# Weight halves split one block sooner at three passages, and the last head's sum of squares moved up behind a quarter of the first output half

## The chip and the metric

The kernel runs on one core of a Trainium2 chip. PE (TensorE) multiplies, ACT (ScalarE), DVE (VectorE) and POOL (GpSimd) do the elementwise work, and SP issues most transfers. Each engine works through its own instructions in order and waits on semaphores for the others. The metric is the device time of one execution in microseconds, median of three runs. The profile gives each engine's records in time, the granted clock of PE, and what ended each wait.

## What is computed

Two transformer blocks on a `[512, 1024]` fp32 activation. The first block is a hybrid mixer (gated linear attention with four heads, plus banded attention) and a feed-forward part; the second has an attention and pooling mixer and then a convolution mixer. The change touches four joints of this chain:

```python
o_a = o_a * lax.rsqrt(jnp.mean(o_a * o_a, axis=-1, keepdims=True) + NORM_EPS)   # per GLA head
o_a = (o_a.reshape(B, L, ...) * jax.nn.silu(ga)).astype(u.dtype)
mix = jnp.concatenate([o_a, o_s], axis=-1) @ w_out                              # output halves
h = h + rmsnorm(mix, norm_mix_post)                                             # first passage
z = rmsnorm(h, norm_mlp_pre) @ w_up
ff = jnp.square(jax.nn.relu(z)) @ w_down
h = h + rmsnorm(ff, norm_mlp_post)                                              # second passage
...
y = even_mixer(rms_norm(x, pre_norm[0]), ...)
x = x + rms_norm(y, post_norm[0])                                               # third passage
h = rms_norm(x, pre_norm[1]); proj = h @ w_in                                   # odd mixer
```

## The kernel before

**Products in three parts.** Every fp32 operand is split into a high part (fp32r) and the rest: `a*b` becomes three matmuls, hi by hi, lo by hi, hi by lo (`mm3`, L702 to L704). So every weight chunk has to pass ACT (`hi`, L1362: `wh` from `wl`) and then DVE (`lo`, L1768: `wlr = wl - wh`). A weight chunk is 1024 rows by 512 columns and comes in two pieces of four 128-row tiles; each piece is one transfer of 1 MB, one ACT copy and one DVE subtraction. Two slots of buffers alternate, chunk `n` in slot `n % 2`; a slot is loaded again when the chunk two before it has been multiplied. PE waits for a piece in `weights(n, half)`, before the first matmul that reads it.

**Tiles.** 512 tokens are four blocks of 128. A tile of a chunk is 24 matmuls of 512 columns: 12 for half 0 (tiles k 0 to 3), 12 for half 1.

**Output of the first mixer.** `w_out` is multiplied in two chunks, `N_O0` and `N_O1`. Its input has eight row tiles: 4 to 7 come from the banded attention and are there early, 0 to 3 are the four GLA heads. So `N_O0` runs half 1 for all four blocks first (48 matmuls), then half 0. Head 3 is the last to be finished: ACT squares it into `sq`, PE adds the squares over the channels with a matmul of ones (`gla_sum(3)`, L912, result in `ps7`), ACT makes the inverse root with Ln and Exp (`head_scale(3)`, L1507, L1508, into `eb`), DVE scales (`gla_normed(3)`, L1989), ACT applies Silu to the four gates `ga` (L1541, which needs another table than Ln and Exp), DVE multiplies (L2011), ACT copies out the high half `act_hi` (`halves`, L1356), and DVE subtracts the low half `act_lo` (L1738). PE's half 0 waits for these low halves, tile by tile. After the Silu the kernel loads the Ln/Exp table again (`exp_ln_tables`, L1305).

**A passage** is the stretch in which a chunk's output becomes the input of the next stage: `s` is 0, 1, 2 for the first mixer to the feed-forward part, that part to the second mixer, and the second mixer to the third. Per block `b`, ACT (`boundary_blocks`) runs `half_square` (L1376: sum of squares of the second output half), `post_scale` (L1383, L1385), `pre_scale` (L1391 to L1396: sum of squares of the new residual) and `hi_turned` (L1403: high half of the transposed block). DVE runs `half_gained` (L1778 or L1780), `new_resid` (L1795), `lo_turned` (L1812) and `normed` (L1804: the block `un`), in the second passage also `add_down` (L1825). PE transposes the normed block (`turn_block`, L840) between halves of its tiles: blocks 0 and 1 in tiles 2 and 3 of the old chunk, blocks 2 and 3 in tiles 0 and 1 of the new one (in the third passage blocks 2 and 3 stand ahead of the new chunk). In `psT` there is room for one turned block, so `turn_block(s, b)` also waits for `lo_turned(s, b - 1)`. In the same loops both engines split the first chunk of the next stage (`following`): ACT its two pieces in blocks 1 and 2, DVE in blocks 2 and 3. The loop order written in the source is the order of the engine.

```python
if b in (1, 2):                # ACT, before: behind post_scale, ahead of pre_scale
    hi(following, b - 1)
if b >= 2:                     # DVE, before: behind new_resid, ahead of lo_turned
    lo(following, b - 2)
```

Of the kernel before, what the change touches and what calls it, by code (L numbers as in the profile page):

```python
# [209 lines left out]
def block_kernel(nc, a, out):  # L210
    ctx = ExitStack()
    with ctx:
# [45 lines left out]
        o1 = m1("o1", [P, KT, TOK])  # L258
# [440 lines left out]
        def _(pe):  # L699
# [397 lines left out]
            pe.wait_ge(evac_done, E_END)  # L1097
            for half in (1, 0):
                weights(N_O0, half)
                if half == 0:  # L1100
                    gla_sum(3)
                for b in range(NBLK):
                    for k in range(4 * half, 4 * half + 4):
                        if b == 0:
                            pe.wait_ge(act_lo_done, 8 + (k - 4 if half else 4 + k) + 1)
                        last = mm3(acc[:, b, :], act_hi[:, k, b * P:(b + 1) * P], act_lo[:, k, b * P:(b + 1) * P],
                                   wh[0][:, k, :], wlr[0][:, k, :], half == 1 and k == 4, half == 0 and k == 3)
                    if half == 0:
                        last.then_inc(wtile_done, 1)
# [190 lines left out]
        def _(act):  # L1300
# [105 lines left out]
            def boundary_blocks(s, following):  # L1406

                for b in range(NBLK):
                    half_square(s, 1, b)
                    post_scale(s, b)  # L1410
                    if b in (1, 2):
                        hi(following, b - 1)
                    pre_scale(s, b)
                    if b >= 1:
                        hi_turned(s, b - 1)
                hi_turned(s, NBLK - 1)
# [122 lines left out]
            head_scale(3)  # L1539
            for h in range(4):  # L1540
                act.activation(ga[:, h, :], ga[:, h, :], ACT.Silu).then_inc(silu_done, 1)  # L1541
            exp_ln_tables()
            halves(o1, (0, 1, 2, 3), lambda e, k: e.wait_ge(og_gated, k + 1))

            hi(N_O1, 0)
            hi(N_O1, 1)
# [163 lines left out]
        def _(dve):  # L1710
# [116 lines left out]
            def boundary_blocks(s, following):  # L1827

                for b in range(NBLK):
                    if s == 1:  # L1830
                        add_down(3, 1, b)
                    half_gained(s, 1, b)
                    new_resid(s, b)
                    if b >= 2:
                        lo(following, b - 2)
                    if b >= 1:
                        lo_turned(s, b - 1)
                    normed(s, b)
                lo_turned(s, NBLK - 1)
# [389 lines left out]
```

## Time and profile before

| | |
|---|---|
| runs before | 1124.20, 1126.48, 1126.49 us; median 1126.48 |
| profiled execution | 1125.93 us, of which the span of the core is 1124.1 |
| PE busy | 1033.6 us, 92% of the span, 4847 matmuls |
| DVE, ACT, POOL busy | 52%, 42%, 15% |
| mean granted PE clock | 0.96 of full speed |
| PE's longest waits | 10.8 us at the start, 7.4 ending at 25.6, 7.6 at 259.8, 4.4 at 667.5, 5.6 at 874.4, 4.3 at 1064.7 |

How to read it: the span runs from the first to the last instruction; 1.8 us lie around it. A row of the timeline gives start, duration, engine, line, operation and names; what stands in brackets is how long the engine was idle before it and what ended the idle time. A matmul record is longer than the distance to the next start, since matmuls are pipelined. The granted clock has two levels, 1.2 GHz (0.5) and 2.4 GHz (1.0); a record of a 512-column matmul is 0.39 us long at the higher and 0.63 us at the lower one. First output half 0 begins at 259.78 us; the first passage lies at 279 to 312 us, the second at 639 to 677, the third at 848 to 878.

### The profile page before, as it was taken

How to read it: one execution, taken by the hardware profiler on the slowest of the kernel's cores; microseconds unless marked ns; L12 is line 12 of the kernel's file. 1: busy time of each engine (PE TensorE's matmuls, PEld its weight loads, DVE VectorE, ACT ScalarE, POOL GpSimd, SP SyncE). 2: the span in 40 equal slices, each digit the busy share in tenths (PEclk: the TensorE clock that was granted, in tenths of full speed). 3: DMA queues.
4: the chain of work that ended last, by engine and by line, in shares of the span. 5: the costliest groups of instructions: out<-in, count | busy, mean ns of one | idle time of the engine just before them, and what ended most of it. 6: DMA issues, size and time to landing. Idle time of an engine off the chain costs nothing.

```text
span 1124.1 us, 12285 instructions
## 1 busy us (share of the span) xinstructions
PE 1033.6 (92%) x4847; PEld 824.7 (73%) x4847; DVE 584.4 (52%) x768; ACT 468.5 (42%) x765; POOL 170.0 (15%) x131
## 2 busy tenths in 40 slices
PE   3899999997999999999999979989898899979897
PEld 2677677886788888888888868767677667657676
DVE  5436665235744234333344463366556397777853
ACT  3325562135533334134123354234355557556541
POOL 2200101000000000000000000022000189886300
PEclk8999999998999999999999999989999799999989
DMA  6532102034221252233224214302033222210301
GB/s 213 73 122 76 38 1 76 1 113 150 76 76 75 75 187 75 75 109 116 76 75 149 76 38 132 141 1 75 2 136 120 68 76 76 75 54 27 145 1 75
DMA packets 55823, 93.91 MB, mean 84 GB/s; under 512 B 2581, under 2 KB 23958, under 8 KB 55638
## 3 DMA queue, kind: packets, MB, share of 16 engines
q1 hardware_dynamic: 53648, 90.61, 23.3%
q10 hardware_dynamic: 2118, 2.52, 1.6%
q8 instruction: 39, 0.64, 0.2%
q14 instruction: 18, 0.15, 0.0%
HBM read 90.76 MB, written 2.36 MB: 83 GB/s over the span
## 4 chain that ended last, share of the span: by engine, by line
PE 55%; DVE 8%; ACT 4%; issue 3%; POOL 1%; DMA 1%; SPq 0%; DVEq 0%; POOLq 0%; ACTq 0%
PE acc L702 17%; PE acc L703 17%; PE acc L704 16%; DVE wlr L1768 2%; ACT wh L1362 2%; DVE psT L2113 1%; POOL pacc L1295 1%; PE psT L861 1%; DMA wl<-in_c_w_in_dram 1%; PE ps L861 1%; PE ps L993 1%; DVE rt L1795 1%; DVE act_lo L1812 1%; ACT junk L1391 1%; PE psT L978 1%
## 5 line engine op out<-in xcount | busy, mean ns | idle before, releaser
L1768 DVE TENSOR_TENSOR wlr<-wl,wh 128x2048 fp32r<-128x2048 f32 (+1 forms) x66 | 149.9, 2276 | 96.4 <-ACT wh L1362 96.4
L702 PE MATMUL acc<-act_hi,wh 128*128 128x512 f32 x464 | 187.9, 405 | 1.7 <-DVE act_lo L1812 1.4
L704 PE MATMUL acc<-act_hi,wlr 128*128 128x512 f32 x464 | 182.3, 393 | 0.0
L703 PE MATMUL acc<-act_lo,wh 128*128 128x512 f32 x464 | 182.1, 392 | 0.0
L1362 ACT ACTIVATE wh<-wl 128x2048 fp32r<-128x2048 f32 (+1 forms) x66 | 123.7, 1880 | 61.2 <-DMA wl<-in_w_up_dram 35.1
L702 PE MATMUL acc<-wh,act_hi 128*128 128x512 f32 x320 | 131.3, 410 | 19.0 <-DVE act_lo L1738 7.6
L703 PE MATMUL acc<-wlr,act_hi 128*128 128x512 f32 x320 | 127.6, 399 | 0.0
L704 PE MATMUL acc<-wh,act_lo 128*128 128x512 f32 x320 | 127.6, 399 | 0.0
L1295 POOL TENSOR_TENSOR pacc<-pacc,prod 128x512 f32<-128x512 f32 x80 | 117.5, 1469 | 28.6 <-ACT prod L1644 16.1
L702 PEld LDWEIGHTS acc<-act_hi,wh 128*128 128x128 f32 x464 | 88.4, 191 | 21.7 <-DVE act_lo L1812 1.8
L703 PEld LDWEIGHTS acc<-act_lo,wh 128*128 128x128 f32 x464 | 88.3, 190 | 19.1 <-issue 1.7
L704 PEld LDWEIGHTS acc<-act_hi,wlr 128*128 128x128 f32 x464 | 87.9, 190 | 19.0
L703 PE MATMUL acc<-wlr,hid_hi 128*128 128x512 f32 x256 | 100.8, 394 | 0.0
L702 PE MATMUL acc<-wh,hid_hi 128*128 128x512 f32 x256 | 100.5, 393 | 0.0
L704 PE MATMUL acc<-wh,hid_lo 128*128 128x512 f32 x256 | 99.4, 388 | 0.0
L702 PEld LDWEIGHTS acc<-wh,act_hi 128*128 128x128 f32 x320 | 61.9, 194 | 34.9 <-DVE act_lo L1738 9.3
L702 PE MATMUL acc<-act_hi,w_hi 128*128 128x512 f32 x152 | 65.5, 431 | 10.8 <-DVE act_lo L1730 7.4
L1276 POOL MEMSET uu<- 128x64 f32 x1 | 0.2, 157 | 475.5 <-PE acc L704 475.5
L703 PEld LDWEIGHTS acc<-wlr,act_hi 128*128 128x128 f32 x320 | 62.3, 195 | 13.0 <-issue 0.7
L704 PEld LDWEIGHTS acc<-wh,act_lo 128*128 128x128 f32 x320 | 61.9, 193 | 13.5
L1644 ACT ACTIVATE prod<-glu,taps 128x512 f32<-128x512 f32 x88 | 60.0, 716 | 13.7 <-POOL pacc L1295 13.0
L2113 DVE SCALAR_TENSOR_TENSOR psT<-glu,taps,psT 128x512 f32<-128x512 f32 x83 | 59.7, 750 | 4.7 <-PE psT L861 4.4
(221 smaller groups left out, 1536.8 us busy)
## 6 DMA issues: line engine op xcount, KB each, us to landing
wl<-in_w_up_dram SPq DMA_DIRECT2D x16, 1024.0 KB, 6.3
wl<-in_w_down_dram SPq DMA_DIRECT2D x16, 1024.0 KB, 6.3
raw<-in_w_in_dram SPq DMA_DIRECT2D x18, 512.0 KB, 4.8
wl<-in_a_w_in_dram SPq DMA_DIRECT2D x8, 1024.0 KB, 6.2
wl<-in_c_w_in_dram SPq DMA_DIRECT2D x16, 512.0 KB, 6.2
wl<-in_w_out_dram SPq DMA_DIRECT2D x4, 1024.0 KB, 6.2
wl<-in_ab_w_out_dram SPq DMA_DIRECT2D x4, 1024.0 KB, 7.4
wl<-in_c_w_in_dram SPq DMA_DIRECT2D x4, 1024.0 KB, 6.4
```

Source lines behind the costliest of these rows:

```text
L702: pe.matmul(dst, hi, x_hi, start=first, stop=False)
L703: pe.matmul(dst, hi, x_lo, start=False, stop=False)
L704: return pe.matmul(dst, lo, x_hi, start=False, stop=last)
L861: last = pe.matmul(vacc(t, 0), diag[:, t % 2, m, :], glu[:, t % 4, j:j + TOK], start=m == 0, stop=m == PE_TAPS - 1)
L978: last = pe.transpose(psTf[:, (2 * b + j) * P:(2 * b + j + 1) * P], LG[layer][:, i % 2, j, 1 + b * P:1 + (b + 1) * P], ident[:, :])
L993: last = pe.matmul(ps6[:, 64 * j:64 * j + 64], PT[layer][:, (2 * b + j) * P:(2 * b + j + 1) * P], VTOK[layer][:, kb, 64 * g:64 * g + 64], ...
L1295: pool.tensor_tensor(pacc[:, t % 2, :], pacc[:, t % 2, :], prod[:, g % 4, :], ALU.add)\
L1362: act.activation(wh[slot][:, kk, cols], wl[slot][:, kk, cols], ACT.Copy).then_inc(whi_done, 1)
L1391: act.activation(junk[:, :], rt[:, b, :], ACT.Square, accum_out=ssq[:, s, 16 + b:17 + b])\
L1644: act.activation(prod[:, g % 4, :], glu[:, t % 4, j:j + TOK], ACT.Copy, scale=taps[:, t, j:j + 1])\
L1768: dve.tensor_tensor(wlr[slot][:, kk, cols], wl[slot][:, kk, cols], wh[slot][:, kk, cols].bitcast(F32), ALU.subtract).then_inc(wlo_done, 1)
L2113: ins = dve.scalar_tensor_tensor(out=sums, in0=src, scalar=taps[:, t, m:m + 1], in1=sums, op0=ALU.mult, op1=ALU.add)
```

## The change

Three edits.

1. PE: `gla_sum(3)` stood between half 1 and half 0 of `N_O0`, behind 48 matmuls. It now stands inside half 1, behind the 12 matmuls of block 0; 36 matmuls that ran ahead of it now run behind it (in PE's instruction order it goes from row 667 to row 631).
2. ACT: the reload of the Ln/Exp table behind the four Silu now stands behind the four `act_hi` copies.
3. At the three passages, ACT copies piece 0 of the next chunk in block 0 (ahead of `pre_scale` in the first two, behind it in the third) and piece 1 in block 1; DVE subtracts them in blocks 1 and 2. Before, it was blocks 1 and 2 for ACT, 2 and 3 for DVE.

No instruction is added or taken away.

```diff
             for half in (1, 0):
                 weights(N_O0, half)
-                if half == 0:
-                    gla_sum(3)
                 for b in range(NBLK):
+                    if half == 1 and b == 1:
+                        gla_sum(3)
...
                     post_scale(s, b)
-                    if b in (1, 2):
-                        hi(following, b - 1)
+                    if b == 1 or (b == 0 and s < 2):
+                        hi(following, b)
                     pre_scale(s, b)
+                    if b == 0 and s == 2:
+                        hi(following, 0)
...
+            halves(o1, (0, 1, 2, 3), lambda e, k: e.wait_ge(og_gated, k + 1))
             exp_ln_tables()
-            halves(o1, (0, 1, 2, 3), lambda e, k: e.wait_ge(og_gated, k + 1))
...
                     new_resid(s, b)
-                    if b >= 2:
-                        lo(following, b - 2)
+                    if b in (1, 2):
+                        lo(following, b - 1)
```

In the changed file every line of ACT's and DVE's parts behind L1412 is two higher.

ACT at the end of the first mixer, from the Ln and Exp of head 3 (`eb`) to the split of `N_O1` (`wh1`), before:

```order
L1507 ACTIVATE eb_85<-ps7,eps_60 128x512
L1508 ACTIVATE eb_85<-eb_85 128x512
L1541 ACT_TABLE_LOAD
L1541 ACTIVATE ga_65<-ga_65 128x512 x4
L1305 ACT_TABLE_LOAD
L1356 ACTIVATE act_hi_53<-o1_61 128x512 x4
L1362 ACTIVATE wh1_140<-wl1_136 128x2048 x2
```

and in the changed kernel:

```order
L1509 ACTIVATE eb_85<-ps7,eps_60 128x512
L1510 ACTIVATE eb_85<-eb_85 128x512
L1543 ACT_TABLE_LOAD
L1543 ACTIVATE ga_65<-ga_65 128x512 x4
L1356 ACTIVATE act_hi_53<-o1_61 128x512 x4
L1305 ACT_TABLE_LOAD
L1362 ACTIVATE wh1_140<-wl1_136 128x2048 x2
```

The table load of L1305 has gone behind the four copies of the heads' high halves and stands directly ahead of the copies of `N_O1`.

ACT in the first passage, blocks 0 and 1 (`wh0` is the next chunk, `junk` of `acc` is `half_square`, `junk` of `rt` is `pre_scale`), before:

```order
L1383 ACTIVATE stat_134<-stat_134 128x1
L1385 ACTIVATE stat_134<-stat_134 128x1
L1391 ACTIVATE junk_124,stat_134<-rt_115 128x1024
L1394 ACTIVATE stat_134<-stat_134,eps_60 128x1
L1396 ACTIVATE stat_134<-stat_134 128x1
L1376 ACTIVATE junk_124,stat_134<-acc 128x512
L1383 ACTIVATE stat_134<-stat_134 128x1
L1385 ACTIVATE stat_134<-stat_134 128x1
L1362 ACTIVATE wh0_139<-wl0_135 128x2048
L1391 ACTIVATE junk_124,stat_134<-rt_115 128x1024
L1394 ACTIVATE stat_134<-stat_134,eps_60 128x1
```

and in the changed kernel:

```order
L1376 ACTIVATE junk_124,stat_134<-acc 128x512 x5
L1383 ACTIVATE stat_134<-stat_134 128x1
L1385 ACTIVATE stat_134<-stat_134 128x1
L1362 ACTIVATE wh0_139<-wl0_135 128x2048
L1391 ACTIVATE junk_124,stat_134<-rt_115 128x1024
L1394 ACTIVATE stat_134<-stat_134,eps_60 128x1
L1396 ACTIVATE stat_134<-stat_134 128x1
L1376 ACTIVATE junk_124,stat_134<-acc 128x512
L1383 ACTIVATE stat_134<-stat_134 128x1
L1385 ACTIVATE stat_134<-stat_134 128x1
L1362 ACTIVATE wh0_139<-wl0_135 128x2048
```

Block 0 has gained a copy ahead of its `pre_scale`; block 1 keeps one at the same place, now that of piece 1; block 2 (not shown) has lost its copy.

DVE in the first passage, from `new_resid` of block 1 (L1795) to the `lo_turned` that block 3 runs, before:

```order
L1795 SCALAR_TENSOR_TENSOR rt_115<-yg_116,stat_134,rt_115 128x1024
L1812 TENSOR_TENSOR act_lo_54<-psT,act_hi_53 128x4x128 x2
L1804 SCALAR_TENSOR_TENSOR un_125<-rt_115,stat_134,gpre_121 128x1024
L1780 TENSOR_TENSOR yg_116<-acc,gpost_120 128x512
L1795 SCALAR_TENSOR_TENSOR rt_115<-yg_116,stat_134,rt_115 128x1024
L1768 TENSOR_TENSOR wlr0_137<-wl0_135,wh0_139 128x2048
L1812 TENSOR_TENSOR act_lo_54<-psT,act_hi_53 128x4x128 x2
L1804 SCALAR_TENSOR_TENSOR un_125<-rt_115,stat_134,gpre_121 128x1024
L1780 TENSOR_TENSOR yg_116<-acc,gpost_120 128x512
L1795 SCALAR_TENSOR_TENSOR rt_115<-yg_116,stat_134,rt_115 128x1024
L1768 TENSOR_TENSOR wlr0_137<-wl0_135,wh0_139 128x2048
L1812 TENSOR_TENSOR act_lo_54<-psT,act_hi_53 128x4x128 x2
```

and in the changed kernel:

```order
L1797 SCALAR_TENSOR_TENSOR rt_115<-yg_116,stat_134,rt_115 128x1024
L1770 TENSOR_TENSOR wlr0_137<-wl0_135,wh0_139 128x2048
L1814 TENSOR_TENSOR act_lo_54<-psT,act_hi_53 128x4x128 x2
L1806 SCALAR_TENSOR_TENSOR un_125<-rt_115,stat_134,gpre_121 128x1024
L1782 TENSOR_TENSOR yg_116<-acc,gpost_120 128x512
L1797 SCALAR_TENSOR_TENSOR rt_115<-yg_116,stat_134,rt_115 128x1024
L1770 TENSOR_TENSOR wlr0_137<-wl0_135,wh0_139 128x2048
L1814 TENSOR_TENSOR act_lo_54<-psT,act_hi_53 128x4x128 x2
L1806 SCALAR_TENSOR_TENSOR un_125<-rt_115,stat_134,gpre_121 128x1024
L1782 TENSOR_TENSOR yg_116<-acc,gpost_120 128x512
L1797 SCALAR_TENSOR_TENSOR rt_115<-yg_116,stat_134,rt_115 128x1024
L1814 TENSOR_TENSOR act_lo_54<-psT,act_hi_53 128x4x128 x2
```

The two subtractions of the next chunk (`wlr0`) each stand one block earlier; block 3 has none now, and its `lo_turned` follows `new_resid` directly.


## Rows read from the trace of the kernel before

**Rows 1.** Waits of PE, whole span: total us, times, longest us.
```profile
PE acc L702 <- DVE act_lo L1738: 7.6, 1, 7.6
...
PE acc L702 <- DVE wlr L1768: 7.0, 3, 4.4
```

**Rows 2.** Timeline of PE, output halves: start us, us, engine, line [idle before <-releaser].
```profile
239.18 1.12 PE L912 MATMUL ps<-sq,ident_ones 128*128 128x512 f32 x2
...
240.38 0.40 PE L703 MATMUL acc<-wlr,act_hi 128*128 128x512 f32 x1
...
242.99 0.39 PE L702 MATMUL acc<-wh,act_hi 128*128 128x512 f32 x1
...
251.15 1.02 PE L912 MATMUL ps<-sq,ident_ones 128*128 128x512 f32 x2
259.78 0.80 PE L702 MATMUL acc<-wh,act_hi 128*128 128x512 f32 x1 [7.61 <-DVE act_lo L1738]
...
265.68 0.40 PE L704 MATMUL acc<-wh,act_lo 128*128 128x512 f32 x1
```

**Rows 3.** Timeline of ACT in the same stretch.
```profile
252.21 0.69 ACT L1507 ACTIVATE eb<-ps,eps 128x512 f32<-128x512 f32 x1 [10.26 <-PE ps L912]
...
257.08 1.28 ACT L1305 ACT_TABLE_LOAD   x1
...
262.22 3.70 ACT L1362 ACTIVATE wh<-wl 128x2048 fp32r<-128x2048 f32 x2
```

**Rows 4.** Timeline of DVE in the same stretch.
```profile
259.03 0.69 DVE L1738 TENSOR_TENSOR act_lo<-o,act_hi 128x512 fp32r<-128x512 f32 x1 [2.09 <-ACT act_hi L1356]
...
261.57 1.48 DVE L1738 TENSOR_TENSOR act_lo<-o,act_hi 128x512 fp32r<-128x512 f32 x2
```

**Rows 5.** Timeline of PE, first passage.
```profile
299.71 1.03 PE L840 MATMUL psT<-ident_ones,un 128*128 128x128 f32 x8
303.11 0.79 PE L702 MATMUL acc<-wh,act_hi 128*128 128x512 f32 x1 [2.37 <-DVE wlr L1768]
303.70 0.63 PE L703 MATMUL acc<-wlr,act_hi 128*128 128x512 f32 x1
...
310.19 1.03 PE L840 MATMUL psT<-ident_ones,un 128*128 128x128 f32 x8
```

**Rows 6.** Timeline of DVE, first passage.
```profile
289.67 1.29 DVE L1812 TENSOR_TENSOR act_lo<-psT,act_hi 128x512 fp32r<-128x512 f32 x2 [2.38 <-ACT act_hi L1403]
...
300.77 2.29 DVE L1768 TENSOR_TENSOR wlr<-wl,wh 128x2048 fp32r<-128x2048 f32 x1
...
304.32 1.28 DVE L1804 SCALAR_TENSOR_TENSOR un<-rt,stat,gpre 128x1024 f32<-128x1024 f32 x1
```

**Rows 7.** Timeline of ACT, first passage.
```profile
281.88 1.06 ACT L1391 ACTIVATE junk<-rt 128x1024 f32<-128x1024 f32 x1 [1.57 <-DVE rt L1795]
```

**Rows 8.** Tile wl, issues between 273 and 274 us: time to landing.
```profile
DMA to landing us min/median/max: 5.3/5.3/5.3
```

**Rows 9.** Timeline of PE, second passage.
```profile
659.20 0.47 PE L702 MATMUL acc<-wh,act_hi 128*128 128x512 f32 x1 [1.86 <-issue]
...
662.05 1.04 PE L840 MATMUL psT<-ident_ones,un 128*128 128x128 f32 x8
667.49 0.50 PE L702 MATMUL acc<-wh,act_hi 128*128 128x512 f32 x1 [4.40 <-DVE wlr L1768]
...
674.70 1.04 PE L840 MATMUL psT<-ident_ones,un 128*128 128x128 f32 x8
```

**Rows 10.** Timeline of DVE, second passage.
```profile
660.48 1.27 DVE L1804 SCALAR_TENSOR_TENSOR un<-rt,stat,gpre 128x1024 f32<-128x1024 f32 x1
...
668.70 1.28 DVE L1804 SCALAR_TENSOR_TENSOR un<-rt,stat,gpre 128x1024 f32<-128x1024 f32 x1
```

**Rows 11.** Timeline of ACT, third passage.
```profile
853.22 0.60 ACT L1376 ACTIVATE junk<-acc 128x512 f32<-128x512 f32 x1 [0.90 <-PE acc L704]
```

**Rows 12.** Timeline of PE, third passage.
```profile
874.41 1.97 PE L840 MATMUL psT<-ident_ones,un 128*128 128x128 f32 x8 [5.64 <-DVE un L1804]
```

## Prediction

> **What bounds the kernel now.** First the busy shares: PE is busy 92% of the span, so whatever shortens the kernel has to shorten PE's matmuls or its waits. Then PE's list of waits [rows 1]: the one wait for a low half of the heads (`act_lo`, 7.6 us) and the three for the low part of a weight chunk (`wlr`, 7.0 us) are the entries that the change aims at. The list says who ended a wait, not what comes next, so the third view is the timeline of PE around each of them, and of ACT and DVE beside it. There the reader is to see three places, and at each how long PE stands still, how long it then runs at the lower clock level, and what would be late next.
>
> **Output halves.** PE ends the 48 matmuls of half 1 at 251.15, runs the sum of squares of head 3, and half 0 starts only at 259.78 [rows 2]. ACT had been idle for 10.26 us before 252.21, waiting for just that sum [rows 3]. So head 3 has been squared by 241.95, while PE passes the new place, the start of block 1 of half 1, at 242.99: the sum doesn't wait there. It starts 251.15 - 242.99 = 8.16 us sooner, and the chain behind it (Ln, Exp, Silu, gating, halves) goes with it, as ACT and DVE do nothing else in this stretch. The table load of 1.28 us stood between Silu and the first half [rows 3]; behind the halves it takes itself out of this chain. The first low half ended at 259.03 + 0.69 = 259.72 [rows 4] and comes at 259.72 - 8.16 - 1.29 = 250.3; the last ended at 263.05 [rows 4] and comes at 253.6.
>
> What does PE do then? A sum of squares and the first matmul behind it took 239.18 to 240.38, 1.20 us [rows 2]. Half 0 so has its second matmul at 251.15 + 1.20 = 252.35, at the higher level one each (251.15 - 242.99)/36 = 0.227 us, and its 15th at 252.35 + 13 x 0.227 = 255.30. Before, that was at 265.68, because the first 12 ran at the lower level [rows 2]. The gain is **10.4 us**. The last low half (253.6) is needed by the 10th matmul at 252.35 + 8 x 0.227 = 254.2: 0.6 us to spare, so the halves don't stop PE, but narrowly. Had the table load stayed, the last half would come at 254.9 and cost 0.7; that is what the second edit is worth.
>
> Next in line are the copies of `N_O1`, 3.70 us [rows 3], behind the moved table load. Their start moves by 8.16 (the load stays ahead of them), to 254.1; with the two subtractions of 2.29 us behind the second copy's 257.8, the weights are split at about 260.5. PE wants them when half 0 ends, 255.30 + 34 x 0.227 = 263.0. They are covered by 2.5 us. The cost of that part is nothing; if the cover were gone, each us more would be one on the path. The residual's load is released by the last low half and moves with it, so it keeps its distance from the weights' load behind it on SP's queue.
>
> **First passage.** PE transposes block 2 at 299.71 (0.79 us to the next start), then needs piece 1 of the next chunk. Its subtraction starts at 300.77 [rows 6], and PE goes on at 303.11 [rows 5]. One block sooner that subtraction stands where piece 0 stood, over 6 us earlier. For piece 0, DVE has the 2.38 us before 289.67 in which it only waits for ACT [rows 6], and a subtraction is 2.29 us long: it fits, by 0.1. On ACT, block 0 had 1.57 us of idle time ahead of `pre_scale` [rows 7]; the copy takes 1.85 (half of 3.70, [rows 3]), so block 0 is some 0.3 late, and PE takes its transposes only at the next break between halves: taken as nothing. So PE continues at 300.50 and has 24 matmuls, 5.44 us, to the transposes of block 3: 305.95 where it was 310.19 [rows 5]. What is late next is `un` of block 3, done at 304.32 + 1.28 = 305.6 [rows 6], since ACT's part of its chain doesn't change: just in time. Gain **4.2 us**: 2.6 of standing still, 1.6 of the 0.63 us matmuls behind it.
>
> Could the early copy wait for its data? The next chunk's load is issued at 273.6, when `N_O0` ends, and piece 0 lands after 5.3 us [rows 8], at 278.9. ACT reaches the copy at 281.88 - 1.57 = 280.3. Cover: 1.4 us. The two events hang on the same end of `N_O0`, so the distance stays.
>
> **Second passage.** Here PE stops twice, 1.86 us before 659.20 and 4.40 before 667.49 [rows 9], for piece 0 (the page's "issue", but DVE ends that subtraction at 659.0) and for piece 1. Both vanish, but here every block's chain over DVE and ACT is longer than PE's work, and the wait that is next is near. New chunk from 657.1 on; 12 matmuls to 659.9; block 2's `un` is only ready at 660.48 + 1.27 = 661.75 [rows 10]: PE waits 1.9 and transposes at 661.8 (662.05 before). Then 24 matmuls without a break to 668.1, and a wait for `un` of block 3, 668.70 + 1.28 = 669.98 [rows 10]. Transposes of block 3 at 670.0 against 674.70 [rows 9]: gain **4.7 us**. DVE's chain isn't shortened by taking the subtraction out of block 3: `lo_turned` waited for ACT's high half there as well.
>
> What is unknown is PE's clock behind these two new waits. In this trace a stop of 1.86 us left it at the higher level (records of 0.47 us and less behind 659.20), and one of 2.37 brought it to the lower one (0.79, then 0.63) [rows 5, 9]. The new stops are 1.9 and 1.9. Bounds: nothing, or behind the second 12 matmuls at 0.427 instead of 0.227, 2.4 us; behind the first it is swallowed by the second wait. I take nothing, since 1.86 is the nearest row, and keep 2.4 for the range. The Trainium skill, TensorE: Matmul & The Clock Gate, Part 1: The HAM clock gate, says that the same kernel shows 6, 11 or 14 slow matmuls at a start from run to run. By that page, 6 to 14 matmuls at the lower level are an estimate of 1.2 to 2.8 us where the level falls at all, and the profiled run need not show what the timed runs do; the trace of before agrees in so far as 7 to 12 matmuls were slow behind its stops.
>
> **Third passage.** Here PE never waited for `wlr`; it waits 5.64 us for `un` [rows 12]. The early copy (1.85) on ACT stands ahead of block 1's `half_square`, where ACT had 0.90 idle [rows 11]. The other 0.95 less a small turnaround, **0.9 us**, delays block 1, and from there on the chain half_square, residual, `pre_scale`, `hi_turned`, `lo_turned`, `un`, next block has no slack, as DVE runs without a break in blocks 1 to 3. Block 1 loses; block 2 is free of ACT's copy, but ACT there waited for DVE anyway. Bounds: 0 to -1.0; I take -0.9.
>
> **Sum.** 10.4 + 4.2 + 4.7 - 0.9 = 18.4 us. On the profiled execution, 1125.93 - 18.4 = 1107.5; it stands 0.55 under the median of 1126.48, so the median of the changed kernel should be **1108.1**. All other stages follow PE and shift as a whole.
>
> **Rivals.**
> - *The clock falls in the second passage.* For: two stops of 1.9 us with 0.8 us of transposes behind each, and 2.37 did it. Against: 1.86 didn't. It gives 1108.1 + 2.4 = 1110.5. Chance 0.22.
> - *Half 0 is not freed.* The sum moves, but the gating chain doesn't follow it, or its cover of 0.6 us fails so that PE still stops about as long there. For: the margin is thin. Against: ACT's 10.26 us of waiting. At worst 1108.1 + 10.4 = 1118.5. Chance 0.06.
> - *Slower: the copy ahead of `pre_scale` waits for its transfer.* ACT's queue is in order, so a late piece 0 holds `pre_scale` and all behind it, then DVE and PE. Place: block 0 of each passage. Price: one us for each us that the piece is later than its cover (1.4 us in the first passage, about the same in the others, and 2 more of slack behind it in the first). With x us more than the 5.3 of [rows 8] it costs (x - 3.4) + 2 (x - 1.4); that passes 18.4 at x = 8.2, a landing of 13.5 us, and at 16 us (x = 10.7) gives 1108.1 + 25.9 = 1134. Against: nothing else is on the transfer engines then. Chance 0.02.
> - *It does nothing measurable*, as other waits take the places: 1126.5. Chance 0.02.
>
> **Numbers.** The forecast, 1108.1 within 1.5 us, has 0.68. The range takes it, the clock rival, and 2 us of spread as the runs before show (1124.2 to 1126.5): 1105.5 to 1112.5, which leaves out a bit under 0.2. A measurement can tell 0.2%, 2.3 us. Faster by more 0.96, within 0.02, slower 0.02.
>
> **What would show it.** In the changed profile: the sum of squares at 243, no stop of PE between 244 and 300 and no 0.63 us records there; the first passage without a stop, transposes of block 3 within 6.3 us of those of block 2; in the second, two stops of 1.9 us, now ended by `un`; in the third, the long stop ends 0.9 us later relative to the stage's start. Wrong would be: a stop ended by `act_lo` or `wlr` at any of these places, ACT waiting for `wl` in a block 0, or 0.63 us records in the second passage.

## The result, and the profile after

The changed kernel took **1105.12 us** (median of 4 runs, 1104.72 to 1105.30) beside 1125.34 (4 runs, 1124.13 to 1126.49) for the kernel before: a ratio of 0.982, 95% interval 0.9803 to 0.9837. Forecast were 1108.1, with a range of 1105.5 to 1112.5. So the sign and most of the size were right, and the time is 0.4 us below the range. The profiled execution took 1105.18 us, 20.75 less than that of before; 18.4 were forecast.

PE's list of waits, first lines (engine, tile, line, releaser: total us, times, longest us):

```profile
PE psT L840 <- DVE un L1806: 11.4, 5, 5.6
...
PE acc L702 <- DVE wlr L1770: 0.3, 1, 0.3
```

Beside [rows 1]: the wait of 7.6 us for `act_lo` has no line any more, and that for `wlr` fell from 7.0 us in three to 0.3 in one. The wait for `un` grew instead, from 7.3 us in three times to 11.4 in five.

**Output halves** (answers [rows 2]), timeline of PE: start us, us, engine, line, [idle before <-releaser]:

```profile
243.05 1.02 PE L912 MATMUL ps<-sq,ident_ones 128*128 128x512 f32 x2
243.50 0.80 PE L702 MATMUL acc<-wh,act_hi 128*128 128x512 f32 x1
244.13 0.40 PE L703 MATMUL acc<-wlr,act_hi 128*128 128x512 f32 x1
...
252.32 0.39 PE L703 MATMUL acc<-wlr,act_hi 128*128 128x512 f32 x1
...
255.26 0.39 PE L704 MATMUL acc<-wh,act_lo 128*128 128x512 f32 x1
```

The sum is at 243.05, and no stop and no 0.63 us record follows. Half 0 has its second matmul at 252.32 and its 15th at 255.26, where before it stood at 265.68 [rows 2]. On ACT and DVE beside it (answer [rows 3, 4]):

```profile
248.87 1.14 ACT L1356 ACTIVATE act_hi<-o 128x512 fp32r<-128x512 f32 x2
...
252.82 1.28 ACT L1305 ACT_TABLE_LOAD   x1
254.12 3.72 ACT L1362 ACTIVATE wh<-wl 128x2048 fp32r<-128x2048 f32 x2
```

```profile
252.05 1.48 DVE L1740 TENSOR_TENSOR act_lo<-o,act_hi 128x512 fp32r<-128x512 f32 x2
```

The last low half ends at 253.53, and the copies of `N_O1` begin at 254.12 behind the table load.

**The passages** (answer [rows 5, 9, 12]): transposes of blocks 2 and 3, one pair for each passage.

```profile
289.27 1.03 PE L840 MATMUL psT<-ident_ones,un 128*128 128x128 f32 x8
...
295.61 1.04 PE L840 MATMUL psT<-ident_ones,un 128*128 128x128 f32 x8
```

```profile
647.29 1.09 PE L840 MATMUL psT<-ident_ones,un 128*128 128x128 f32 x8 [1.63 <-DVE un L1806]
648.13 0.48 PE L702 MATMUL acc<-wh,act_hi 128*128 128x512 f32 x1
655.51 1.09 PE L840 MATMUL psT<-ident_ones,un 128*128 128x128 f32 x8 [1.64 <-DVE un L1806]
656.35 0.48 PE L702 MATMUL acc<-wh,act_hi 128*128 128x512 f32 x1
```

```profile
847.63 1.09 PE L840 MATMUL psT<-ident_ones,un 128*128 128x128 f32 x8 [1.98 <-DVE un L1806]
854.37 1.75 PE L840 MATMUL psT<-ident_ones,un 128*128 128x128 f32 x7 [5.64 <-DVE un L1806]
```

The first has no stop. The second has two, ended by `un`, and the first record behind each is 0.48 us long, so the clock stayed at its higher level. In the third the long stop is as long as before, 5.64 us, but comes later in its stage: block 2's stop ahead of it is 1.98 us long where the kernel before had 1.19.

**Where 20.7 us went.** The start of one PE instruction in the trace of before, less its start in that of after, is what has been gained up to there:

| landmark on PE | before | after | gained so far | this stage | forecast |
|---|---|---|---|---|---|
| first transposes (L840) | 287.03 | 276.58 | 10.45 | 10.5 | 10.4 |
| block 3, first passage | 310.19 | 295.61 | 14.58 | 4.1 | 4.2 |
| block 3, second passage | 674.70 | 655.51 | 19.19 | 4.6 | 4.7 |
| first output matmul of the second mixer | 819.95 | 799.12 | 20.83 | **1.6** | 0 |
| block 3, third passage | 874.41 | 854.37 | 20.04 | -0.8 | -0.9 |
| last transposes | 1087.23 | 1066.50 | 20.73 | **0.7** | 0 |

In this pair of traces every stage that the change touches came out within 0.1 us of its term. In part that is luck of the pair: a repeat of the kernel before, further down, divides its time otherwise. What the forecast lacks is in two stretches that it does not touch. The larger is the second mixer, between the second passage and its own output matmuls, 145.25 us before and 143.61 after. I call it **the stretch**, and its length is the main reading in what follows.

The same part of it in both kernels, first a window of 13 us, then the next 39 to 41 us. Behind the window's length stand PE's busy us, its instructions, the granted clock, the DMA share and GB/s. Before:

```profile
738.40:751.40 13.00, 8.56 (x39) 0.82 0.00 1
751.40:792.00 40.60, 38.53 (x215) 0.97 0.15 52
```

After:

```profile
719.00:732.00 13.00, 9.16 (x42) 0.87 0.00 1
732.00:771.00 39.00, 37.10 (x212) 1.00 0.15 55
```

Behind the 13 us the changed kernel ran at 1.00 for 39 us, the kernel before at 0.97 in its 40.6. It is the same work; what differs is where the level falls. Of the 0.7 us behind the third passage, 0.3 stand at two matmuls at the end of a stretch at the lower level (0.63 and 0.45 us long in the trace of before, 0.40 in that of after), and the rest is scattered in steps of 0.1 us or less.

### The profile page after: what moved, and what is told of

The parts are those of the page before. It is cut to its first block, busy times and chain, and to the rows that moved or that the text cites. A ratio compares the mean times of both kernels' runs of the same rounds, so it can differ in the third digit from the quotient of the medians.

```text
span 1103.4 us, 12286 instructions
## 1 busy us (share of the span) xinstructions
PE 1024.3 (93%) x4847; PEld 818.9 (74%) x4847; DVE 585.8 (53%) x768; ACT 468.1 (42%) x765; POOL 170.3 (15%) x131
## 3 DMA queue, kind: packets, MB, share of 16 engines
HBM read 90.76 MB, written 2.36 MB: 84 GB/s over the span
## 4 chain that ended last, share of the span: by engine, by line
PE 68%; DVE 10%; ACT 5%; issue 3%; POOL 1%; DMA 1%; SPq 0%; DVEq 0%; POOLq 0%; ACTq 0%
PE acc L702 19%; PE acc L703 19%; PE acc L704 19%; ACT wh L1362 2%; PE ps L993 2%; DVE wlr L1770 2%; DVE psT L2115 1%; POOL pacc L1295 1%; PE psT L1079 1%; PE psT L861 1%; DMA wl<-in_c_w_in_dram 1%; PE ps L861 1%; PE psT L978 1%; PE acc L967 1%; PE psT L840 1%
## 5 line engine op out<-in xcount | busy, mean ns | idle before, releaser
L702 PE MATMUL acc<-wh,act_hi 128*128 128x512 f32 x320 | 128.9, 403 | 2.8 <-DVE act_lo L1814 2.8
```

The costliest lines, as they stand in the source:

```text
L702: pe.matmul(dst, hi, x_hi, start=first, stop=False)
```

## The experiments

### The parts alone

**a1_sum_only** has edit 1 alone, on the kernel before:

```diff
                 weights(N_O0, half)
-                if half == 0:
-                    gla_sum(3)
                 for b in range(NBLK):
+                    if half == 1 and b == 1:
+                        gla_sum(3)
```

> Kernel before with only the last head's sum of squares moved up behind a quarter of the first output half; the table load stays ahead of the halves, the passages are as before. Theory (the forecast's first term): the chain of head 3 starts 8.16 us sooner, the stop of 7.6 us and the lower clock behind it go, less 0.7 us because the last low half then comes at 254.9 where PE wants it at 254.2: 9.7 us less than before, 1125.3 - 9.7 = 1115.6. Rival (the table load matters more): each of the four low halves comes too late, PE stops four times and the clock falls again: 6 to 8 us less, about 1118.

Measured: 1115.62 us (1114.86 to 1116.54) beside 1124.95, ratio 0.9918 (0.9904 to 0.9931), as expected.

**a2_sum_table** adds edit 2 (`exp_ln_tables()` behind `halves`).

> As the first kernel of this call, and the table load behind the halves: the whole first term. Theory: 10.4 us less than before, 1114.9, and 0.7 less than with the sum alone. Rival (the table load is worth its full 1.28 us or nothing): 1.3 less than the first kernel, or the same. The trace of the changed kernel shows the term at 10.5 us at the start of the first passage.

Measured: 1115.81 us (1113.68 to 1116.22), ratio 0.9915 (0.9902 to 0.9929), where 1114.9 were expected. The times can't separate the two, the traces can: from the sum to the first transposes (L840) PE took 34.52 us in a1 (242.72 to 277.24) and 33.53 in a2 (243.22 to 276.75), the same 33.53 as in the changed kernel. The table load is worth 1.0 us here, 0.7 were expected. It was lost again in the first passage, whose stop both still have. In a1:

```profile
293.32 0.50 PE L702 MATMUL acc<-wh,act_hi 128*128 128x512 f32 x1 [2.37 <-DVE wlr L1768]
293.66 0.39 PE L703 MATMUL acc<-wlr,act_hi 128*128 128x512 f32 x1
```

and in a2:

```profile
292.84 0.56 PE L702 MATMUL acc<-wh,act_hi 128*128 128x512 f32 x1 [2.36 <-DVE wlr L1768]
293.20 0.63 PE L703 MATMUL acc<-wlr,act_hi 128*128 128x512 f32 x1
293.63 0.63 PE L704 MATMUL acc<-wh,act_lo 128*128 128x512 f32 x1
```

A stop of 2.37 us left the clock up, one of 2.36 was followed by the lower level. So the length of a stop does not decide that by itself. Nor does the kernel, as r_before_again shows further down.

**a3_passages_only** has edit 3 alone.

> The change of the three passages alone, sum and table as before. Theory (the terms add, the extra gain of 1.6 us between the second and the third passage is a matter of where the clock falls there and not of the edit): 4.1 + 4.7 - 0.8 = 8.0 less, 1117.3, give or take 1.7 for that stretch; its trace shows the shift of PE against before at the second passage's end 8.8 us. Rival (the extra 1.6 us is a true effect of the edits at the passages, work of ACT or DVE that is missing later): 9.6 to 10 less, 1115.5, with DVE's and ACT's rows of the attention stretch nearer to each other than before.

Measured: 1114.94 us (1114.00 to 1115.95), ratio 0.9911 (0.9898 to 0.9925): 10.0 us less than 1124.95, the rival's number and not my sum of 8.0. Its stretch is 143.64 us, that of a1 145.33 and of a2 145.23. So in this trace the 1.6 us come with edit 3, though it touches nothing in there. With a1 the two make 9.3 + 10.0 = 19.3 of the 20.2 between the medians; edit 2 is in neither.

**a4_third_as_before** is the changed kernel without edit 3 in the third passage:

```diff
-                    if b == 1 or (b == 0 and s < 2):
-                        hi(following, b)
+                    if (b in (1, 2) if s == 2 else b < 2):
+                        hi(following, b - 1 if s == 2 else b)
                     pre_scale(s, b)
-                    if b == 0 and s == 2:
-                        hi(following, 0)
...
-                    if b in (1, 2):
-                        lo(following, b - 1)
+                    if b >= 2 if s == 2 else b in (1, 2):
+                        lo(following, b - 2 if s == 2 else b - 1)
```

> The changed kernel with the third passage put back as it was before (ACT's copies in blocks 1 and 2, DVE's subtractions in blocks 2 and 3), the first two as changed. Theory: the third passage lost 0.75 us through ACT's copy ahead of block 1's sum of squares; without it 1105.1 - 0.75 = 1104.4, and the last stop of that passage begins and ends 0.8 us sooner after the start of its stage. Rival (the loss there is paid back, since the transposes wait anyway): 1105.1, no difference.

Measured: 1105.16 us (1105.10 to 1105.72), ratio 0.9825 (0.9812 to 0.9839), no different from the changed kernel. From the first output matmul to the transposes of block 3 it took 54.47 us, as before, and not 55.25: the 0.8 us are real. But its stretch was 146.54 us, 2.9 more than in the first trace of the changed kernel, and from the transposes of block 3 to the last ones it took 210.25 us and not 212.13, 1.9 less. Most of that stands at one group of eight products (L861) of the convolution mixer, behind a stop of the same length. In a4:

```profile
938.39 3.70 PE L861 MATMUL ps<-glu,diag 128*128 128x512 f32 x8 [2.04 <-DVE glu L2093]
```

and in the changed kernel:

```profile
937.08 5.40 PE L861 MATMUL ps<-glu,diag 128*128 128x512 f32 x8 [2.05 <-DVE glu L2095]
```

The granted clock between 934 and 946 us was 1.00 in a4 and 0.86 in the changed kernel. So the 0.8 us were gained, and differences of the clock larger than that hid them.

### What sets the length of the stretch

Delayed kernels have 4, 8 or 12 extra matmuls, whose result isn't used, at the start of the stretch:

```diff
+                if n == N_KV and m == 0 and half == 0:
+                    for _ in range(8):
+                        pe.matmul(acc[:, TILES[e][2], :], wh[n % 2][:, 0, col:col + P], act_hi[:, 0, :],
+                                  start=True, stop=True)
```

First both kernels unchanged, and both with 8 matmuls (1.8 us):

> The changed kernel once more, unchanged, for another trace. Open is the 1.6 us that its first trace gained between the second and the third passage, where no edit lies: from the transposes of block 3 of the second passage to the first output matmul of the second mixer 143.6 us, against 145.2 in the kernel before. Theory (the place at which PE's clock falls among many short stops differs from run to run): the stretch comes out anywhere between 143.5 and 146.5 us in this trace, with slow matmuls at other places. Rival (it belongs to the edits of the passages): 143.6 again, the slow matmuls at the same place, 47 us ahead of the end of the stretch or so.

> The kernel before once more. Theory (the clock differs from run to run): its times scatter over some 3 us as in the runs so far, its stretch between the second and third passage takes something else than 145.2 us, and the numbers of slow matmuls behind its stops at 303 and 667 us differ from the 6 and 7 of the first trace. Rival: the trace repeats to 0.1 us.

> The changed kernel with 8 more matmuls of 512 columns in a row ahead of the first tile of keys and values of the second mixer (the first product is computed 8 times more and overwritten, the output is the reference's), 8 x 0.227 = 1.8 us of PE. Theory (run to run): the delay adds itself, 1105.1 + 1.8 = 1106.9, and the stretch is 1.8 us longer than in some other run. Rival (the gain hangs on when this stretch begins, as set by the edits): shifted by 1.8 us the gain is lost or changed, 1108.5 or 1105.5.

> The kernel before with the same 8 matmuls more, 1.8 us. Theory (run to run): 1125.0 + 1.8 = 1126.8. Rival (the kernel before meets the clock at a bad moment in this stretch because of when it begins): the delay is partly or wholly paid back, 1125.2, as the fall lands where PE waits anyway.

Measured: r_after_again 1104.78 (1103.96 to 1109.10), stretch 143.65; r_before_again 1126.83 (1125.03 to 1127.52), stretch 145.60; d_after_8 1110.6 (1107.50 to 1110.73), ratio 0.9856 (0.9842 to 0.987), stretch 147.37, which is 145.55 without its extra matmuls; d_before_8 1127.8 (1125.22 to 1130.13), ratio 1.0016 (1.0007 to 1.0025), stretch 148.26, so 146.44. The traced execution of d_after_8 was the fastest of its four, 1107.50; the other three took 3.1 us more, which no trace places, and their median is above both forecasts. d_before_8 is 1.7 us above the 1126.15 beside it: the delay added itself, and the rival, 1125.2, fails.

The repeat of the kernel before answered what its expectation asked. Its stretch is nearly the old one, but at the first passage, where the first trace has 0.79 and then 0.63 us behind a stop of 2.37 [rows 5], it has:

```profile
304.31 0.50 PE L702 MATMUL acc<-wh,act_hi 128*128 128x512 f32 x1 [2.36 <-DVE wlr L1768]
304.65 0.39 PE L703 MATMUL acc<-wlr,act_hi 128*128 128x512 f32 x1
```

One program, the same stop, and another level. From the first transposes to block 3 of the first passage the kernel before so took 23.16 us in its first trace and 21.66 in this one, while the changed kernel took 19.03 and 19.04 in its first two traces. The repeat lost that time elsewhere: its level fell at 240 us, ahead of the sum of squares, which cost 1.5 us, and its second passage had 0.9 us more.

The short stretch came back in the changed kernel and was gone with a delay of 1.8 us. I then held that the kernel sets the place, and asked whether other delays give other lengths:

> The changed kernel with 4 more matmuls of 512 columns (0.9 us) ahead of the first tile of the second mixer; their result isn't used. 8 such matmuls (1.8 us) made the stretch from the second passage's last transposes to the first output matmul 147.37 instead of 143.6, so 1.9 more than they last. Theory (the place where the level falls goes by when the stretch begins): any length between 144.5 and 148 is possible, and its slow matmuls stand elsewhere than at 722. Rival (the stretch has two lengths and a threshold): 144.5, or 146.4. Total 1106.0 or up to 1109.5.

> As d_after_4 with 12 more matmuls (2.7 us). If the 1.6 us depend only on the stretch beginning early enough, it stays lost: 143.6 + 2.7 + 1.9 = 148.2, total 1109.7. If the place of the fall goes round with the time of the beginning, the stretch less its 2.7 us differs from the 145.5 of 8 matmuls by over 0.5 either way.

Measured: d_after_4 1108.02 (1104.76 to 1109.22), stretch 147.32, so 146.41; d_after_12 1111.50 (1110.03 to 1113.07), stretch 147.91, so 145.18. (Its total is so high because from the transposes of block 3 of the third passage to the last ones it took 215.08 us, 2.9 more than d_after_8; there PE waited 4.43 us for DVE's `ct` at 978 us where the changed kernel waits 3.04.) With 4 matmuls it was neither of the two lengths that a threshold would give, and with 12 it stayed within 0.4 of the 145.5 of 8, short of the 0.5 that would have shown the place going round with the time. Neither theory gained by it. But one of the four executions of d_after_4 took 1104.76, 2.9 us less than the next. That led to the opposite question, whether one kernel has both lengths:

> The changed kernel again, unchanged. Its nine timed executions so far lie at 1104.0 to 1105.3 (seven) and at 1107.6 and 1109.1 (two). Theory A (the place where PE's level falls in the second mixer is set by the kernel): the stretch from the second passage's last transposes to the first output matmul is again 143.6. Theory B (it differs from execution to execution, and the two profiled ones fell alike): about one trace in four shows another length, 145 or more, and its execution takes 1107 or more. This trace: 143.6 under A, 143.6 or 145 to 147 under B, and its time must follow.

> As r_after_3, one more execution of the changed kernel. Theory A: stretch 143.6, time about 1105. Theory B: 143.6 with 1104 to 1105, or 145 to 147 with 1107 or more.

> The kernel of d_after_4 again: its four executions took 1109.2 (the profiled one, stretch 147.3), 1108.4, 1107.7 and 1104.8. Theory A: stretch 147.3 again. Theory B: in some executions it is the short 143.6 + 0.9 = 144.5, which is the 1104.8; here either 147.3 with 1108 to 1109 or 144.5 with about 1105 to 1106.

> The kernel before with 4 more matmuls (0.9 us) ahead of the first tile of the second mixer. Two traces of the kernel before have a stretch of 145.25 and 145.60, the one with 8 more matmuls 148.26, which is 146.4 without them. Theory (the length goes by where the level falls, in the kernel before too): 144.5 to 148, and not just 145.4 + 0.9 = 146.3 at another place of the fall. Rival (only kernels with the new second passage can have other lengths): 146.3 within 0.3. Time 1125.5 to 1129.

Measured: **r_after_3 took 1110.04 us with a stretch of 146.38; r_after_4 1104.83 with 143.71.** Both are the changed kernel, unchanged. d_after_4_again took 1107.55 with 147.07. d_before_4 took 1127.82 (1125.23 to 1130.57), ratio 1.0023 (1.0007 to 1.0039), stretch 145.75, so 144.84. Theory B holds: the kernel does not set the length alone. The kernel before has other lengths too, 0.25 beyond the rival's bound for d_before_4. Of the 5.2 us between r_after_3 and r_after_4, 2.7 lie in the stretch. Another 2.3 lie ahead of the last sum of squares (244.81 against 242.55 us), 1.3 of them at the slow matmuls that only r_after_3 has from 239.8 to 242.5 us. The two forms of the stretch side by side, timeline of PE. The changed kernel, first trace:

```profile
722.34 0.69 PE L978 MATMUL psT<-ident_ones,lg 128*128 128x128 f32 x2 [0.82 <-ACT lg L1442]
722.68 0.78 PE L702 MATMUL acc<-act_hi,wh 128*128 128x512 f32 x1
723.26 0.63 PE L703 MATMUL acc<-act_lo,wh 128*128 128x512 f32 x1
...
726.74 0.40 PE L704 MATMUL acc<-act_hi,wlr 128*128 128x512 f32 x1
727.57 0.63 PE L993 MATMUL ps<-v_tok,pT 128*128 128x64 f32 x4 [0.43 <-DVE oq L1891]
...
731.74 0.48 PE L702 MATMUL acc<-act_hi,wh 128*128 128x512 f32 x1
```

The same instructions in r_after_3:

```profile
724.07 0.44 PE L978 MATMUL psT<-ident_ones,lg 128*128 128x128 f32 x2 [0.82 <-ACT lg L1442]
724.26 0.48 PE L702 MATMUL acc<-act_hi,wh 128*128 128x512 f32 x1
724.58 0.40 PE L703 MATMUL acc<-act_lo,wh 128*128 128x512 f32 x1
...
729.29 0.63 PE L993 MATMUL ps<-v_tok,pT 128*128 128x64 f32 x4 [2.05 <-DVE oq L1891]
730.56 0.79 PE L967 MATMUL acc<-k,q 64*128 64x256 f32 x1 [0.64 <-DVE lg L1876]
...
734.23 0.78 PE L702 MATMUL acc<-act_hi,wh 128*128 128x512 f32 x1
734.80 0.63 PE L703 MATMUL acc<-act_lo,wh 128*128 128x512 f32 x1
```

The part ends with a wait for DVE's `oq` in either case, 5.2 us behind the L978 row. In the first trace the level falls ahead of that wait: seven matmuls are long, and only the idle time shrinks, from 2.05 to 0.43 us. Behind it the clock is up. In r_after_3 the matmuls ahead of the wait are short, PE idles 2.05 us, and the level is low behind it, where nothing covers it: against r_after_4 it is 2.2 us behind when the wait ends and 4.5 us behind once its level is up again. The kernel before does what r_after_3 does:

```profile
746.72 1.09 PE L993 MATMUL ps<-v_tok,pT 128*128 128x64 f32 x4 [2.03 <-DVE oq L1889]
...
751.66 0.78 PE L702 MATMUL acc<-act_hi,wh 128*128 128x512 f32 x1
752.24 0.63 PE L703 MATMUL acc<-act_lo,wh 128*128 128x512 f32 x1
```

### A version that beats both

The stops left in the second and third passage end with `un`, which DVE makes behind `lo_turned` of the block before. PE needs both. **f1_normed_first** swaps them in all passages; **f2_normed_first_third** also has the third passage of a4.

```diff
                         lo(following, b - 1)
+                    normed(s, b)
                     if b >= 1:
                         lo_turned(s, b - 1)
-                    normed(s, b)
```

> The changed kernel, and in all three passages DVE runs normed(b) ahead of lo_turned(b - 1) instead of behind it. The two stops of PE in the second passage (1.63 and 1.64 us) and the long one in the third end with un, while DVE runs two subtractions of lo_turned (1.29 us together) ahead of it. With un first, PE only waits for the first of the two behind it to free half of psT. From the trace of the changed kernel: block 3 of the second passage, pre_scale ready at 652.4, un at 653.7, first lo_turned at 654.3: transposes at 654.4 where they began at 655.51, 1.1 sooner; third passage, pre_scale at 851.3, un at 852.6, first lo_turned at 853.2: transposes 1.1 sooner than 854.37. Theory: 2.2 us, 1105.1 - 2.2 = 1102.9. Rival 1: PE has to wait for lo_turned anyway and the transposes come no sooner: 1105.1. Rival 2: both transposes come sooner, but the level of PE falls at another place of the second mixer and the stretch behind the second passage goes from 143.6 back to 145.5: 1104.8. The place of the transposes and the length of the stretch tell the three apart.

> The kernel of f1_normed_first, with the third passage's weight halves split as in the kernel before the change (ACT blocks 1 and 2, DVE blocks 2 and 3). In the changed kernel that edit shortened the third passage by 0.79 us (55.26 to 54.47 from the first output matmul to the transposes of block 3) but the total stayed the same, as the level of PE fell elsewhere. Theory: 0.8 less than f1_normed_first, 1102.1. Rival: same total as f1_normed_first within 0.5, with a stretch behind the second passage over 144.5.

Measured: f1 1105.28 us (1104.42 to 1106.58), ratio 0.982 (0.9807 to 0.9834), like the changed kernel; f2 **1101.54** us (1100.38 to 1102.63), ratio 0.9783 (0.977 to 0.9796). In f1's trace the transposes now wait for `act_lo`:

```profile
645.69 1.16 PE L840 MATMUL psT<-ident_ones,un 128*128 128x128 f32 x8 [1.40 <-DVE act_lo L1814]
653.42 1.17 PE L840 MATMUL psT<-ident_ones,un 128*128 128x128 f32 x8 [1.11 <-DVE act_lo L1814]
```

Counted from the sum of squares, those of block 3 are at 410.98 us where the changed kernel has 412.46: 1.5 sooner. In the third passage they are 53.85 us behind the first output matmul and not 55.25: 1.4 sooner. But the stretch was 145.28 us (+1.7) and the three stages behind the third passage were 1.1 us longer, so nearly nothing was left: rival 2. f2 had the same longer stretch (145.55) and a third passage of 53.18 us, 0.7 less than f1. Its median is 3.7 us below that of f1 where 0.8 was expected. What the traces add is in the stages behind: 210.58 us against 213.19, 2.6 less, with the same group of L861 at 3.70 us again, as in a4, and at 5.40 in f1. So most of the step from f1 to f2 lies where no edit is, and its stretch over 144.5 us, the rival's sign, came without the rival's total. To see whether f2 is better when both run on one chip:

> The changed kernel again, on the same chip as r_f2_again. Of its eleven executions so far eight took 1103.96 to 1105.30 and three 1107.55 to 1110.04; traces of the first kind have a stretch of 143.6 to 143.7 us, the one of the second kind 146.38. Expected: the same two groups, three or four in the lower one, median about 1105; the traced one follows its group.

> The kernel of f2_normed_first_third again (normed ahead of lo_turned, third passage's weight halves as before the change). It took 1101.54 beside 1125.54; the changed kernel took 1105.12 beside 1125.34 in another comparison. If the 3.6 us between them are real, the median here is 1101.5 within 1, 3 to 4 us below r_after_5. Rival (the two happened to fall on different places of the clock): within 1.5 us of r_after_5.

Measured: r_after_5 1104.54 us (1104.20 to 1105.55), ratio 0.9815 (0.9801 to 0.9828); r_f2_again 1101.33 us (1100.95 to 1102.37), ratio 0.9785 (0.9771 to 0.9798). f2 is 3.2 us faster than the changed kernel; all five executions of r_after_5 were of the lower group. The traced one had a stretch of 143.98. Against it the trace of r_f2_again gained 1.5 us up to block 3 of the second passage, lost 1.6 in the stretch, and gained 2.1 in the third passage and 1.8 behind it; 1.6 it had lost ahead of the last sum of squares, where the two kernels don't differ. The 1.5 and the 2.1 are work of the edits. In the 1.8 is a difference of the clock: this one group of L861 took 3.70 us in the three traces of a4, f2 and r_f2_again, and 5.40 in the other 17 traces of this case. Why the level stays up there is not shown, so how much of f2's lead would survive in another kernel isn't either.

The stretch in every trace, without the extra matmuls:

| kernel | stretch, us |
|---|---|
| before, r_before_again, d_before_4, d_before_8 | 145.25, 145.60, 144.84, 146.44 |
| a1, a2 | 145.33, 145.23 |
| a3 | 143.64 |
| after and its repeats | 143.61, 143.65, 143.71, 143.98 and 146.38 |
| a4, f1, f2 and its repeat | 146.54, 145.28, 145.55, 145.57 |
| d_after_4 twice, d_after_8, d_after_12 | 146.41, 146.16, 145.55, 145.18 |

## Why the prediction was wrong by 3 us

**Output halves: right.** Forecast 10.4, measured 10.5. The sum did not wait, ACT's chain followed it, and the second matmul of half 0 (252.35 forecast, 252.32 measured), the 15th (255.30, 255.26), the last low half (253.6, 253.53) and the copies of `N_O1` (254.1, 254.12) came where they were put. The thin cover of 0.6 us held. Without edit 2, in a1, PE loses 1.0 us up to the first transposes where 0.7 was said; the one stop in that trace that the profile puts down to a half is 0.30 us long.

**First passage: right, with luck in the size.** 4.1 for 4.2. No stop, 6.34 us between the transposes of blocks 2 and 3. But 1.6 of the 4.2 were the slow matmuls behind the old stop. They are in three of the six traces that have this stop (before, d_before_8 and a2, from the first transposes to block 3 23.1 to 23.3 us) and not in the others (r_before_again, d_before_4 and a1, 21.66 us). The stop itself is there in all six, and that it went away is no luck.

**Second passage: right, on the clock as well.** 4.6 for 4.7. Two stops, of 1.63 and 1.64 us where 1.9 was forecast, and the level didn't fall behind them. That the nearest row decides (1.86, not 2.37) gave the right answer, and the repeats of the changed kernel have the same two stops and the same level behind them. But the row taken against it was weaker than it looked: in a1 2.37 us did not bring the level down, and in r_before_again 2.36 did not, in the very kernel that the row came from.

**Third passage: right.** -0.8 for -0.9, shown by a4 and by the trace.

**The step that failed** is the sentence "All other stages follow PE and shift as a whole". They follow in their work, but not in PE's clock. In the pair of profiled executions the stretch gave 1.6 us and the stages behind the third passage 0.7; together they are the 2.3 between 20.7 and 18.4. That the 1.6 is a matter of where the level falls is shown by the two kernels' rows and by r_after_3; for the 0.7 the rows show it in 0.3. The term was put at nothing. I had asked of the clock only at stops that the change makes or takes away, and not at the existing short stops behind them.

The first explanation for the 1.6 us, that the edits set the place of the fall, fell too. r_after_3 is the same program with a stretch of 146.38, longer than before the change, and took 1110.04 us. Of 16 executions of the changed kernel 13 took 1103.96 to 1105.55 and three 1107.55, 1109.10 and 1110.04. The forecast of 1107.5 for a profiled execution lies between the two groups. That the short form is frequent in the changed kernel (four of five traces, and the one of a3) and was not seen in six traces with the second passage as before, nor in those of a4, f1 and f2, is counted; why, and what makes the level fall where it does, is not settled. The Trainium skill, TensorE: Matmul & The Clock Gate, Part 1: The HAM clock gate, says that the chip's watching of PE runs freely and does not start anew with a kernel, so that the count of slow matmuls at one kernel's start differs from run to run. r_after_3 beside r_after_4, 5.2 us apart, agree, and show it in the middle of a kernel too. For the ramp at a kernel's start the page gives under 1% of a typical span; no run here singles that ramp out, and the two executions as a whole differ by 0.5%.

**The rest of the miss is the reference point.** The forecast was set on 1126.48, the median of three runs. With the four runs of the comparison it was 1125.34, and in the later ones the kernel before had medians of 1124.95 to 1126.15, as an unchanged repeat 1126.83. My profiled execution of before (1125.93) was closer, and I added 0.55 to go from it to the median. 2.35 of the stages, 0.55 of that step and 0.06 between the profiled execution after and its median make the 3.0 between 1108.1 and 1105.12.

**The range** took its low end from the spread of the three runs before, and left no room for a stage outside the change. With the 2.3 us of the untouched stages, a size known only afterwards, as a cost of unknown sign it would have begun near 1103.

**The rivals.** No `act_lo` stop, no wait of ACT for `wl` in a block 0, and a change that did what it says. The rival on the clock, a fall in the second passage, did not come true either; the clock moved the result by some 2 us, but in another stage, and downwards.

## What to carry to other kernels

When a change shifts a later stage whose engine has short stops, treat PE's clock there as a cost of unknown sign, sized by the difference between two traces of the same kernel. Here that was 2.8 us in one stretch, more than some of the edits. The same holds for a term read from a single trace: the slow matmuls behind a stop, 1.6 us, can be missing from the next execution. An edit worth less than this is judged by distances between two landmarks around it, as a4, a2 and f1 were: their totals said nothing, and the distances did. And a lower clock ahead of a wait for another engine costs nothing while the wait is the longer of the two (it shrank from 2.05 to 0.43 us here); behind the wait it cost its full price, 2.2 us.

## What the runs showed of the hardware

- One kernel on one input, 1104.83 and 1110.04 us: the stretch of 143.71 or 146.38 us goes by the place where the granted level falls, and 2.3 us more lie ahead of the last sum of squares.
- A stop of 2.37 us in the first trace of the kernel before and one of 2.36 in its repeat, at the same instruction: behind one the matmuls were 0.63 us long, behind the other 0.39. All 28 stops of 1.6 to 1.9 us in the second passage (two in each of eleven traces, one in each of six) had a record of 0.48 us or less behind them.
- A group of eight products behind a stop of 2.04 us took 3.70 us in a4, and behind one of 2.05 us 5.40 in the changed kernel.
- Four matmuls more (0.9 us) at the start of the stretch made the changed kernel 2.9 us slower by the medians (1105.12 and 1108.02, in two comparisons).
